# A hybrid attention and recurrence layer on one core: seven attention steps scored between the tiles of V, over a ring of five exponential tiles

## The reference

```python
u = rms_norm(h, g_norm)
z = u @ w_in                       # q, k, v, g_att (512 columns each), xr, g_lru (512 each)
# differential attention, 8 heads, two score maps a head, bidirectional
s = einsum('bqhcd,bkhcd->bhcqk', qblk, kf) + bias[None, :, None]
pr = softmax(s, axis=-1)
w = pr[:, :, 0] - lam * pr[:, :, 1]
o_att = einsum('bhqk,bkhe->bqhe', w, vf)
# recurrence: convolution, gates, two scans
mix = concatenate([rms_norm(o_att) * silu(g_att), o_lru * silu(g_lru)])
h = h + mix @ w_out
e = (p @ w_ple) * sigmoid(h @ w_pg)
h = h + rms_norm(e, g_ple)
```

## Time and profile before

| | |
|---|---|
| Median of three runs | 1044.28 us (1043.69 to 1045.43) |
| Profiled execution | 1045.79 us, of which the span of its records is 1044.0 us |
| PE busy | 1008.5 us (97% of the span), 5792 matmuls |
| DVE busy | 659.5 us (63%) |
| ACT busy | 580.8 us (56%) |
| POOL busy | 500.5 us (48%) |
| V's tiles | 389 to 457 us of the span |
| Attention's loop | 458 to 766 us |
| Granted TensorE clock, mean | 0.994 |

### The profile page before, as it was taken

The page is one execution under the profiler, slowest core; times in us unless marked ns, Lnnn a source line. Parts: engine busy times, 40 slices in busy tenths (PEclk is TensorE's granted clock), DMA queues, the critical chain, the costliest instruction groups (busy, mean ns, idle before and its releaser), DMA issues.

```text
span 1044.0 us, 15464 instructions
## 1 busy us (share of the span) xinstructions
PE 1008.5 (97%) x5792; PEld 800.3 (77%) x5792; DVE 659.5 (63%) x1055; ACT 580.8 (56%) x890; POOL 500.5 (48%) x404
## 2 busy tenths in 40 slices
PE   8999999999999999989999999999999999999997
PEld 6877777767787888857777777777788888888886
DVE  4654958583493250259999999999966244445423
ACT  7738485744641131269999999999952221122112
POOL 1233245526566550036667767766667244354421
PEclk9999999999999999999999999999999999999999
DMA  9651543323255526839687478363285222432221
GB/s 337 241 169 36 172 147 101 116 81 115 77 162 164 159 81 188 243 101 243 167 197 210 110 192 223 82 159 122 68 300 167 86 87 86 137 121 86 100 87 41
DMA packets 105929, 150.34 MB, mean 144 GB/s; under 512 B 10232, under 2 KB 68728, under 8 KB 105848
## 3 DMA queue, kind: packets, MB, share of 16 engines
q1 hardware_dynamic: 105712, 149.36, 47.5%
q10 hardware_dynamic: 144, 0.00, 0.0%
HBM read 102.07 MB, written 44.11 MB: 140 GB/s over the span
## 4 chain that ended last, share of the span: by engine, by line
PE 63%; DVE 19%; issue 10%; ACT 3%; POOL 2%; DMA 2%; SPq 0%; DVEq 0%; POOLq 0%; ACTq 0%
DVE E_ L1638 11%; PE b_ps L1917 5%; PE b_ps L1919 5%; PE b_ps L1918 5%; PE b_ps L1814 4%; PE g_ps L1816 4%; PE g_ps L1814 4%; PE g_ps L1815 4%; PE b_ps L1815 4%; PE b_ps L1816 4%; PE o_ps L1980 3%; PE w_ps L1963 2%; PE h_ps L1814 2%; PE h_ps L1816 2%; PE h_ps L1815 2%
## 5 line engine op out<-in xcount | busy, mean ns | idle before, releaser
L1251 ACT ACTIVATE E_<-E_,nmax 128x1024 f32<-128x1024 f32 (+1 forms) x184 | 186.7, 1018 | 15.0 <-DVE nmax L1638 14.8
L1638 DVE CUSTOM_DVE_ANT_0 E_<-s_ps,bias 128x1024 f32<-128x1024 f32 (+1 forms) x184 | 188.0, 1056 | 3.6 <-PE s_ps L1930 3.6
L969 POOL TENSOR_TENSOR E_<-E_,ratio 128x576 f32<-128x576 f32 (+3 forms) x92 | 84.5, 919 | 85.8 <-DVE E_ L1654 85.8
L1816 PE MATMUL b_ps<-u_hi,wA_lo 128*128 128x512 f32 x288 | 113.3, 394 | 0.0
L972 POOL TENSOR_TENSOR E_<-E_ 128x576 f32<-128x576 f32 (+3 forms) x92 | 103.7, 1127 | 7.2
L1930 PE MATMUL s_ps<-KL,QL 128*128 128x512 f32 x256 | 90.7, 435 | 13.9 <-DVE nmax L1638 13.1
L1814 PE MATMUL b_ps<-u_hi,wA_hi 128*128 128x512 f32 x240 | 96.7, 403 | 5.0 <-DVE u_lo L1410 2.8
L1815 PE MATMUL b_ps<-u_lo,wA_hi 128*128 128x512 f32 x240 | 94.7, 395 | 0.0
L1963 PE MATMUL w_ps<-ident,E_ 128*128 128x128 f32 x624 | 83.4, 273 | 1.8 <-ACT WT L1282 1.7
L1282 ACT ACTIVATE WT<-w_ps 128x1024 f32<-128x1024 f32 (+1 forms) x96 | 83.3, 868 | 2.8 <-PE w_ps L1963 2.6
L1980 PE MATMUL o_ps<-WT,V 128*64 128x128 f32 x1280 | 84.0, 278 | 0.0
(11 more groups left out here) (228 smaller groups left out, 2329.6 us busy)
## 6 DMA issues: line engine op xcount, KB each, us to landing
QL<-qk_t SPq DMA_DIRECT2D x32, 256.0 KB, 6.9
KL<-qk_t SPq DMA_DIRECT2D x32, 256.0 KB, 8.2
bias<-line_d SPq DMA_DIRECT2D x8, 960.0 KB, 11.8
x_sb<-in_x SPq DMA_DIRECT2D x12, 512.0 KB, 9.0
z_ch<-z_stage SPq DMA_DIRECT2D x24, 256.0 KB, 2.7
qk_t<-qh SPq DMA_DIRECT2D x24, 256.0 KB, 2.3
qk_t<-ql SPq DMA_DIRECT2D x24, 256.0 KB, 2.8
mf<-mix_t SPq DMA_DIRECT2D x24, 256.0 KB, 3.8
```

Of the source, the lines that this page charges most:

```text
L1251: act.activation(e, e, ACT.Exp, bias=nmax[:, n % 5, c:c + 1], scale=-1.0, accum_out=sums[:, n % 5, c:c + 1]).then_inc(e_done, 1)
L1638: dve.tensor_tensor_reduce(weights_at(n)[:, c, 0:n_tok], s_ps[:, c, 0:n_tok], b[:, ::-1], -1.0, 3e38, ALU.add, ALU.min, nmax[:, n % 5, c:c ...
L1816: mm = pe.matmul(dst, sl, mh, start=False, stop=k == n - 1)
```

## The change

Scores of seven steps, not four, are made between V's tiles, behind tiles 4 to 10; their maxima follow on DVE, and their exponentials on ACT behind the evacuations of tiles 5 to 11. Steps 4, 5 and 6 are long ones, and factor and combine of steps 0 to 4 are ahead of the loop too. The four splits of output weights on DVE (`wl_low`) stand behind steps 3 and 4 and no longer behind 0 and 1. As long scores need the first bank of `b_ps` (it is the last bank of `s_ps`), V's tiles 3, 6 and 9 go to the first bank of `qT_ps`; tile 3 waits until Q's and K's last transposes have left it. As slot 4 of `E` lies over input that V's last tiles still read, the ring is permuted: step n goes to slot `E_SLOT[n % 5]`, so that steps 4, 5, 6, 7, 8 take slots 2, 3, 1, 0, 4.

In the loops each lead is one longer: PE scores step n+5 in loop n, ACT does the exponentials of n+4, DVE factor and combine of n+3 and biased of n+5. In between (`steps_to`), PE and DVE have steps 7 and 8 in loops 0 and 1, nothing new in loops 2 and 3, step 9 in loop 4, and ACT 7 and 8 in loops 0 and 1 and 9 in loop 5. The ring still has five tiles and the wait at L1635 is unchanged, so that biased(n+5, 0) waits for turn(n). SP's and POOL's orders are unchanged.

```diff
+        E_SLOT = (3, 1, 0, 4, 2)
+
         def weights_at(n):
-            return Es[:, n, :, :] if n < 4 else E[:, n % 5, :, :]
+            return Es[:, n, :, :] if n < 4 else E[:, E_SLOT[n % 5], :, :]
...
+        EARLY, RING = 7, 5
+
+        def steps_to(n, done, lead):
+
+            return min(NSTEP, max(min(done + n + 1, EARLY + 2), n + 1 + lead)) if n >= 0 else done
+
+        def due(n, done, lead):
+
+            return range(steps_to(n - 1, done, lead), steps_to(n, done, lead))
+
+        def v_bank(t):
+
+            return b_ps[:, t % NB, :] if t % NB or not t else qT_ps[:, 0, :, :].rearrange("p a b -> p (a b)")
...
-                act.activation(sq_junk[:, t % 2, :], b_ps[:, t % 3, :], ACT.Copy, scale=rsx[:, t:t + 1]
+                act.activation(sq_junk[:, t % 2, :], v_bank(t), ACT.Copy, scale=rsx[:, t:t + 1]
                                ).then_inc(v_evac, 1)
...
-                if t >= 9:
+                if t >= NT - EARLY:
                     for c in range(2):
-                        exps(t - 9, c)
+                        exps(t - NT + EARLY, c)
...
             for n in range(NSTEP):
                 blk, head, u, qt = STEPS[n]
-                if n + 3 < NSTEP:
-                    exps(n + 3, 0)
+                for m in due(n, EARLY, RING - 1):
+                    exps(m, 0)
                 if qt == 1 and blk:
                     heads_out(blk - 1)
-                if n + 3 < NSTEP:
-                    exps(n + 3, 1)
+                for m in due(n, EARLY, RING - 1):
+                    exps(m, 1)
...
-            for n in range(4):
+            for n in range(EARLY):
                 for c in range(2):
                     biased(n, c)
-                if n < 2:
-                    wl_low(2 * n)
-                    wl_low(2 * n + 1)
+                if n in (3, 4):
+                    wl_low(2 * n - 6)
+                    wl_low(2 * n - 5)
                 if n >= 2:
                     factor(n - 2)
                     combine(n - 2)
             for n in range(NSTEP):
                 blk, head, u, qt = STEPS[n]
-                if n + 2 < NSTEP:
-                    factor(n + 2)
-                    combine(n + 2)
-                if n + 4 < NSTEP:
-                    biased(n + 4, 0)
-                    biased(n + 4, 1)
+                for m in due(n, EARLY - 2, RING - 2):
+                    factor(m)
+                    combine(m)
+                for m in due(n, EARLY, RING):
+                    biased(m, 0)
+                    biased(m, 1)
...
-                dst = b_ps[:, n % NB, :]
+                if g == 2 and t == NB:
+                    pe.wait_ge(qlo_done, 2 * NT - 1)
+                dst = v_bank(t) if g == 2 else b_ps[:, n % NB, :]
...
             for n in range(3 * NT):
                 qkv_tile(n)
-                if 2 * NT + 7 <= n < 2 * NT + 11:
-                    if n == 2 * NT + 7:
+                if 3 * NT - EARLY - 1 <= n < 3 * NT - 1:
+                    if n == 3 * NT - EARLY - 1:
                         pe.wait_ge(sig_done, UNITS_C * LC)
                     for c in range(2):
-                        scores(n - 2 * NT - 7, c)
+                        scores(n - 3 * NT + EARLY + 1, c)
...
-                if n + 4 < NSTEP:
-                    scores(n + 4, 0)
+                for m in due(n, EARLY, RING):
+                    scores(m, 0)
                 turn(n)
-                if n + 4 < NSTEP:
-                    scores(n + 4, 1)
+                for m in due(n, EARLY, RING):
+                    scores(m, 1)
```

## The result

The changed kernel took 1056.88 us (median of four runs, 1053.73 to 1058.14), the kernel before 1044.69 us beside it: ratio 1.0113, 95% interval 1.0088 to 1.0137, so 12 us slower. The prediction had the sign and the places, but 4.8 us and a range that ended at 1052.5.

A forecast was written before the change was run, and what follows sets the result against it. DVE was taken to bound the attention stage, PE the rest. Terms: +0.1 to b(16,0), +0.4 clock, +2.7 cycles, -0.6 and +2.2 at the end: +4.8 on 1044.28, so 1049.1 us; 8-in-10 range 1043.8 to 1052.5.

The forecast's parts named there:

- V's tiles: V's projection tiles: three new long steps' scores add 2.8 us and a wait for K 0.4, so V ends 3.2 later.
- PE's wait for Ks: At the first scores between V's tiles: PE waits 0.4 us for K's last slice, bounds 0 and 1.
- b(7,0) 8.0 us ahead, none of it kept: Ramp behind V: DVE's first bias pass of step 7 starts 8.0 us earlier, but the five-slot ring prevents keeping that.
- Rival (a): Ramp: DVE's head start is kept, 1038 to 1039 us, or half kept, 1041 to 1043; together 0.11.
- The clock: Ramp behind V: PE's idle gaps likely halve TensorE's clock for about 3 us; priced at +0.4 us.
- The second bias: Before step 12's first bias pass: the second head's bias lands late; +1.4 us, bounds 0 and 2.5.
- the walk through turns 0 to 4: Ramp behind V: turns wait for ACT's copies, so step 9's first bias pass starts at 475.1 us.
- The cycles: Twelve-step attention cycles: waits for turns in short steps make 38.65 us from 38.30 or 38.0; +2.7 us, bounds 0 and 5.
- The splits: Four cycles where ACT and POOL split output weights: 38.30 becomes 38.65 us, with no extra term for the splits.
- The end: Last steps: 0.6 us won back by step 95's bias pass, then +2.2 us at the last turns, all showing in the end.
- (c): Ramp clock: forecast without a fall 1048.7 us, with a full fall 1050.7; inside the forecast's range, together 0.60.
- (d): Short stretches of every cycle cost 1.2 us instead of 0.65, seven times: +4 more, 1053 us; chance 0.08.

The follow-up runs named there:

- e3: Changed kernel with POOL's splits of output weights two steps later; ratio 1.0116 to the kernel before.
- e12: Changed kernel with old leads in the loops, ACT's copies first in loops 0 to 4, first Q and K loaded before bias, score maps swapped; ratio 0.9993 to before.
- e5: Changed kernel with ACT's copy of a turn ahead of its exponentials in loops 0 to 4; ratio 1.0086 to the kernel before.
- e4: Changed kernel with idle transposes on PE, which nobody reads, ahead of turns 1 to 4; ratio 1.0104 to the kernel before.
- e7: Changed kernel with ACT's copies of output weights two steps earlier, POOL's splits where they were; ratio 1.0112 to the kernel before.
- e9: Changed kernel with POOL's eight splits of output weights behind its last combine, out of the loop; ratio 1.0151 to the kernel before.
- e13: e4 with the second head's bias issued ahead of its long Q and K; ratio 1.0085 to the kernel before.
- e1: Changed kernel with seven steps still scored between V's tiles but the old leads in the loops; ratio 1.0047 to the kernel before.
- e2: Changed kernel with only four steps scored between V's tiles, but each loop lead one longer; ratio 1.0127 to the kernel before.

## Why the prediction was half right

- **V's tiles.** +3.2 us predicted, +3.8 measured. The twelve matmuls are right: later gaps are 5.92 and 6.39 us. PE's wait for Ks was 0.4 in the sum, with bounds 0 and 1. By the spacing of tiles 4 and 5 (6.86 - 5.92) it was 0.94 us, and 1.8 us in e3, so the upper bound was too low as well. With Q and K loaded first (e12) it is gone.
- **b(7,0) 8.0 us ahead, none of it kept.** Right: 7.4 us ahead, and turns 1 and 2 wait for ACT's copies. Rival (a) falls with the times, and even with the copies first (e5) the 6.6 us ahead at b(7,0) are gone at b(16,0).
- **The clock: the first failed step.** The fall was called likelier than not, its place in the ramp too, and it was priced at +0.4 us, with 3 us at half clock copied from the stretch at 10.5 us. There PE was busy all the time after the gap. In the ramp it isn't: 1.94 of 5 us, and the clock stayed at half for 13.6 us, over turns 1 to 4 and step 9's scores. Measured by e4: 2.85 us. How long it stays is in part luck: the same code gave 10.2 us in e7 and e9, and from V's end the price was 2.2 to 3.0 us.
- **The second bias.** +1.4 us in the sum, 0 in the changed kernel, 0.69 us in e4. Mechanism right, its size half, and covered here by the slower clock. With neither clock nor bias (e13) b(16,0) is at 114.51 us; the prediction's other terms, with V's end as measured, give 114.55 + 0.1 - 1.4 + 0.6 = 113.85. So the walk through turns 0 to 4 was 0.7 us too short as well.
- **The cycles.** 38.65 us predicted, 38.60 and 38.61 measured where nothing is split, with waits of 0.19, 0.49 and 0.79 us before b(14,0), b(15,0) and b(16,0) against 0.1, 0.6 and 0.9 as walked.
- **The splits: the second failed step.** For the four cycles "in which ACT and POOL also split output weights" 38.30 simply became 38.65 us, +0.35, by a walk "with the same durations": what the splits do to DVE was put at nothing. It measured +1.43 us a cycle, 4.3 us more in all. In its place the runs show 1.04 us by which DVE's ratio and combine are stretched beside POOL, as much as before (1.05), but no longer taken up by 0.65 us of waits, as the changed kernel's last wait comes ahead of them; without the splits in the loop (e9) all of it is gone. POOL's queue was never walked, though POOL's combine moved a step ahead of ACT's copy there, and the row of 2.9 us for POOL's waits for `wa_hi` was in the same list as the earlier trace rows. That walk alone would have given where the splits run, and not the price.
- **The end.** b(88,0) to b(95,0) -0.6 and the last turns +2.2 predicted, -0.6 and +2.35 measured; e1 and e2 show that it is the lead. "From turn(93) on PE has no wait left" was wrong by 0.9 us: PE waits 0.49 us for `O_n` (L2056), and every kernel that ends with the long lead loses 0.1 to 1.3 us there (e9, with its splits in that place, 8.4), none with the old lead over 0.1.
- **Together.** 3.6 + 6.9 - 0.6 + 2.4 + 0.9 = 13.1 us against a sum of 4.8. Of the 8.3 missed, the clock is 2.5 and the splits 4.3; V's end (0.6) and the end behind turn(95) (0.9) are nearly all of the rest. Bias (0.6 less than forecast) and walk (0.7 more) cancel. No rival named the splits, and (c) named the clock's full fall, but at 2.0 us and inside the range; (d) had its 4 us in short stretches of every cycle, which measured as in the forecast. The range should have held the full fall of the clock beside every other term, and didn't.

## What to carry to other kernels

A head start made in an idle stage is worth only what the buffers can hold: walk it to the first step that reuses a slot, and see whose turn frees that slot. When one engine's order moves a step ahead, go through every queue that feeds or follows it, small side jobs too, and ask beside which instructions of the bound engine they run and which of its waits behind them can still give way: POOL's splits stretched DVE by 1.05 us a cycle in both kernels, and cost 0.3 us in one and 1.1 us in the other. And price a fall of the clock by the stretch in which it happens, with its own idle time, not by a dense stretch elsewhere.

## What the hardware showed that I had not expected

A small DVE instruction with two inputs in SBUF doesn't slow down beside POOL in proportion to its size, it ends with POOL's instruction. One pair, from the timelines of both engines, is in the ramp of the changed kernel: the ratio, 128x1, takes 1.13 us and not 0.22, and ends at 458.42 us, POOL's multiplication at 458.41.

```profile
457.26 1.15 POOL L985 TENSOR_TENSOR E_<-E_,ratio 128x576 f32<-128x576 f32 x1 [4.81 <-DVE E_ L1670]
457.29 1.13 DVE L1663 SCALAR_TENSOR_TENSOR ratio<-sums,rsum,neglam 128x1 f32<-128x1 f32 x1
```

The same holds for the split: in the rows at 539.89 and 540.58 us above both end at 541.17 and 541.18. Of the changed kernel's 96 ratios 39 take over 0.25 us, and each of these ends within 0.02 us of the end of a POOL instruction that ran when it started; no semaphore of POOL's splits is one that DVE waits for. This is what the Trainium skill's "SBUF — State Buffer" (Who interferes with whom) calls an exclusive lock of the port pair that the two engines share, and the trace agrees. For one such DVE instruction the cost can come near POOL's whole duration, as 1.13 beside 1.15 us shows, however small it is. DVE's bias pass, with one input in PSUM and one in SBUF, takes its usual 1.23 us beside the split at 537.25 us. And the same code ahead of V took 3.3 us more or less from one execution to the next (379.5 to 382.9 us), which is why terms under 1 us were read from a row just ahead of the change and not from the total.
